# One section for the first norm and the input projection, with products behind the row conversion

## What is computed

```python
mod = jax.nn.silu(c) @ w_ada[l] + b_ada[l]
shift1, scale1, gate1, shift2, scale2, gate2 = jnp.split(mod, 6, axis=-1)
h = rms_norm(x, norm1_g[l]) * (1.0 + scale1[:, None, :]) + shift1[:, None, :]
z = h @ w_in[l]
c_q, c_kv, k_pe, dq, dk, dv = jnp.split(z, offsets, axis=-1)
```

## Time and profile before

| | us |
|---|---|
| median of 3 runs | 2666.83 (2664.89 to 2669.32) |
| the profiled execution | 2670.07 |
| its span, first to last instruction | 2668.3 |
| first matmul of the input projection | 71.6 |
| first matmul of unit 4 | 98.4 |
| end of the input projection on PE | about 276 |

### The profile page before, as it was taken

One profiled execution on the slowest core, in us unless ns is written; L12 is line 12 of the kernel. 1 busy time (PEld: TensorE's weight loads), 2 busy tenths in 40 slices (PEclk: granted clock), 3 DMA queues, 4 the chain that ended last, 5 costly groups with the idle time before them and its releaser, 6 DMA issues. The chain is left out here.

```text
span 2668.3 us, 38277 instructions
## 1 busy us (share of the span) xinstructions
PE 2487.0 (93%) x13514; PEld 1988.3 (75%) x13526; DVE 1643.6 (62%) x3033; ACT 1368.0 (51%) x2416; POOL 418.4 (16%) x530
## 2 busy tenths in 40 slices
PE   5999999999996999999994999997999899998999
PEld 4788479788765888888883778885666688886667
DVE  6663455687657999999986545420656546741761
ACT  4253244597345888888875533321666523322850
POOL 0121012320302211111112100000223200000330
PEclk7999899999997999999997999998999999999999
DMA  6642000001229999999976411033111222113211
GB/s 242 189 142 68 0 1 1 1 1 33 97 84 391 411 419 410 420 414 413 413 306 224 158 44 64 24 126 134 33 65 33 85 95 76 32 49 126 80 46 50
DMA packets 128109, 400.26 MB, mean 150 GB/s; under 512 B 12103, under 2 KB 62412, under 8 KB 115550
## 3 DMA queue, kind: packets, MB, share of 16 engines
q1 hardware_dynamic: 114522, 353.30, 35.0%
q0 software_dynamic: 12048, 42.56, 4.0%
q10 hardware_dynamic: 1396, 2.50, 0.3%
HBM read 347.93 MB, written 50.40 MB: 149 GB/s over the span
## 5 line engine op out<-in xcount | busy, mean ns | idle before, releaser
L3070 DVE CUSTOM_DVE_ANT_0 fox_l<-PS,fox_c 128x1024 f32<-128x1024 f32 (+7 forms) x128 | 92.1, 756 | 129.5 <-PE PS L3117 86.8
L3007 ACT ACTIVATE fox_l<-fox_l,stat 128x1024 f32<-128x1024 f32 (+7 forms) x128 | 98.4, 771 | 91.3 <-DVE stat L3070 90.5
L447 PE MATMUL PS<-wehg,xsTh 128*128 128x512 f32 x256 | 100.5, 392 | 3.0 <-ACT xsTh L2736 2.0
L447 PE MATMUL PS<-wehu,xsTh 128*128 128x512 f32 x256 | 103.2, 403 | 0.0
L447 PE MATMUL PS<-wqkh,uTh 128*128 128x512 f32 x256 | 103.1, 403 | 0.0
L449 PE MATMUL PS<-wqkh,uTl 128*128 128x512 f32 x256 | 100.3, 392 | 0.0
L449 PE MATMUL PS<-wehu,xsTl 128*128 128x512 f32 x256 | 100.2, 392 | 0.0
L449 PE MATMUL PS<-wehg,xsTl 128*128 128x512 f32 x256 | 100.2, 391 | 0.0
L448 PE MATMUL PS<-wqk_rest,uTh 128*128 128x512 f32 x256 | 100.0, 391 | 0.0
L449 PE MATMUL PS<-wehd,aTl 128*128 128x512 f32 x248 | 96.5, 389 | 0.0
L447 PE MATMUL PS<-wehd,aTh 128*128 128x512 f32 x248 | 96.5, 389 | 0.0
(11 more groups left out here) (610 smaller groups left out, 7499.1 us busy)
## 6 DMA issues: line engine op xcount, KB each, us to landing
we0g<-in_w_expert_gate SPq DMA_DIRECT2D x16, 2048.0 KB, 10.9
we0u<-in_w_expert_up SPq DMA_DIRECT2D x16, 2048.0 KB
we1g<-in_w_expert_gate SPq DMA_DIRECT2D x16, 2048.0 KB, 11.4
we1u<-in_w_expert_up SPq DMA_DIRECT2D x16, 2048.0 KB
we0d<-in_w_expert_down SPq DMA_DIRECT2D x16, 2048.0 KB
we1d<-in_w_expert_down SPq DMA_DIRECT2D x16, 2048.0 KB
wada_rest<-in_w_ada SPq DMA_DIRECT2D x16, 1024.0 KB, 5.7
X<-in_x SPq DMA_DIRECT2D x16, 512.0 KB, 11.6
```

Of the source, the lines that this page charges most:

```text
L447: nc.tensor.matmul(out, lh, rh, start=start, stop=False)
L3007: nc.scalar.activation(prob(p, e)[:, 0:K], prob(p, e)[:, 0:K], ACT.Exp, bias=nbm[:, u % 8:u % 8 + 1], scale=-1.0, accum_out=rsum[:, u % 16 ...
L3070: nc.vector.tensor_tensor_reduce(out=prob(p, e)[:, 0:K], in0=PS[:, 2 * e:2 * e + 2, :].rearrange("p a b -> p (a b)")[:, 0:K], in1=C[:, h % ...
```

## The change

The two sections become one (`phase_start_and_in`), so that no engine waits for the others between them, and the work in it is put in another order:

- PE no longer turns all rows ahead of the products. It turns units 0 to 3 as before (`FREE` is 4 instead of 6, in banks 4 to 7), and then runs units 0 and 1 (chunks 0 and 1 against the first half of the tokens) together, k by k: six matmuls as soon as unit k of the rows is converted, then `turn` of unit k + 4. The same for the second half. `units` lists the first four accordingly.
- ACT rounds weight chunks 0 and 1 ahead of the conversion of the rows. DVE takes their rests at the start of the conversion (first halves) and after its unit 3 (second halves).
- Loads: `X` tiles 6 and 7 go ahead of `w_ada` chunks 1 to 3, of `mats` only the identity is loaded first and the rest behind the first weight chunks, `trig` and the final gain go to SP behind later waits. `scale(2)` moves from behind chunk 3 to behind chunk 0, and the small lambda and mask operations to behind the conversion.
- Weight chunk 2 has a buffer of its own, where `X` lay, and is loaded as soon as eight units of rows are turned. Pieces 0 to 2 are loaded once all sixteen are turned. Chunks 3 and 4 are loaded after the first four units; then come pieces 3 and 4, and from chunk 5 on each chunk's load stands ahead of one or two pieces. Seven pieces instead of eight run before the rope, and `sum_after` names later units.

```diff
-            for i in range(1, NC):
-                chunk(i)
-            for t in range(6, T):
-                rows(t)
+        for t in range(6, T):
+            rows(t)
+        for i in range(1, NC):
+            chunk(i)
         load(sp, [(env.win[i], env.win_in[i], in_chunks(A)[i][0]) for i in range(2)])
+        sp.dma_start(env.mats[:, P:11 * P], A["mats"][:, P:11 * P]).then_inc(mats_in, 16)
...
-    sum_after = {2: 0, 4: 1, 6: 2, 8: 3, 12: 4, 16: 5, 20: 6, 24: 7}
+    sum_after = {5: 0, 7: 1, 9: 2, 12: 3, 15: 4, 18: 5, 21: 6, 25: 7}
...
-            for q in range(4):
-                ada(q)
-            for c in range(2, NCH):
-                sp.wait_ge(mm, 2 * (c - 1))
+        sp.wait_ge(first["turned"], KD)
+        load_in_chunk(sp, raw[2], chunks[2], second_in)
+        sp.dma_start(env.trig[:, :, :], A["trig"].rearrange("p (a s) -> p a s", a=2)).then_inc(env.trig_in, 16)
+        sp.wait_ge(first["turned"], 2 * KD)
+        for q in range(3):
+            ada(q)
+        sp.wait_ge(mm, 4)
+        for c in range(3, 5):
+            load_in_chunk(sp, raw[c], chunks[c], w_in[c % 2])
+        ada(3)
+        ada(4)
+        sp.dma_start(env.rows[:, 2, :], A["final_norm_g"].partition_broadcast(P)).then_inc(env.trig_in, 16)
+        for c in range(5, NCH):
+            sp.wait_ge(mm, 2 * (c - 1))
...
+        for n in range(2):
+            h = slice(n * HALF, (n + 1) * HALF)
+            for k in range(KD):
+                pe.wait_ge(first["split"], KD * n + k + 1)
+                for c in range(2):
+                    if n == 0 and k % 4 == 0:
+                        pe.wait_ge(w_lo01, 2 * (k // 4) + c + 1)
+                    last = split_product(nc, PS[:, 2 * n + c, :], (wh[c][:, k, :], lo_of(c)[:, k, :]),
+                                         (xh[:, k, h], xl[:, k, h]), k == 0, k == KD - 1)
+                    if k == KD - 1:
+                        last.then_inc(mm, 1)
+                if KD * n + k + first["free"] < 2 * KD:
+                    first["turn"](pe, KD * n + k + first["free"])
```

More of the change, by code:

```diff
@@ new lines, in convert_act @@
+    def convert_act(act):
+        act.wait_ge(mod_ready, 2)
+        for u in range(2 * KD):
+            if u % 2 == 0:
+                a, b = ab(u)
+                act.wait_ge(t_ready, u + 1)
+                nc.scalar.activation(part(full, u), bank(u), ACT.Identity, scale=a, bias=b).then_inc(full_act, 1)
+                act.wait_ge(full_act, u // 2 + 1)
+            else:
+                act.wait_ge(full_dve, u // 2 + 1)
+            nc.scalar.copy(part(hi, u), part(full, u)).then_inc(hi_done, 1)
@@ new lines, in on_pool, with on_act, chunk_hi @@
+    def on_pool(pool):
+        for c in range(2, NCH):
+            for part in range(2):
+                r = slice(4 * part, 4 * part + 4)
+                pool.wait_ge(w_hi, 2 * c + part + 1)
+                nc.gpsimd.tensor_tensor(lo_of(c)[:, r, :], raw[c][:, r, :], wh[c][:, r, :].bitcast(F32),
+                                        ALU.subtract).then_inc(w_lo, 1)
+    def on_act(act):
+        act.dma_start(brow[0:1, 0, :], A["b_ada"][0:1, 2 * D:3 * D]).then_inc(brow_in, 16)
+        act.dma_start(brow[0:1, 1, :], A["b_ada"][0:1, 5 * D:6 * D]).then_inc(brow_in, 16)
+        arrived = [0, 0]
+        def chunk_hi(c):
+            if c == 2:
+                act.wait_ge(second_in, 16 * len(chunks[c]))
+            else:
+                arrived[c % 2] += 16 * len(chunks[c])
+                act.wait_ge(w_in[c % 2], arrived[c % 2])
+            if c > 2:
+                act.wait_ge(mm, 2 * (c - 1))
+            for part in range(2):
+                r = slice(4 * part, 4 * part + 4)
+                nc.scalar.copy(wh[c][:, r, :], raw[c][:, r, :]).then_inc(w_hi, 1)
+        chunk_hi(0)
+        chunk_hi(1)
+        first["convert_act"](act)
+        for u, (kind, c, n) in enumerate(units):
+            act.wait_ge(mm, u + 1)
+            bank = PS[:, u % 4, :]
+            r = u - ROPE0
+            if kind == "c":
+                nc.scalar.copy(place(kind, c, n), bank).then_inc(evac, 1)
+            elif kind == "v":
+                if u < V0 + 2:
+                    act.wait_ge(rope_done, r - 1)
+                else:
+                    act.wait_ge(v_t, u - V0 - 1)
+                nc.scalar.copy(RS[:, r % 2, :], bank).then_inc(evac, 1)
+            else:
+                if r >= 2:
+                    act.wait_ge(rope_done, r - 1)
+                for b in range(4):
+                    to, frm = slice(32 * b, 32 * b + 32), slice(32 * (b ^ 1), 32 * (b ^ 1) + 32)
+                    last = nc.scalar.activation(RS[to, r % 2, :], PS[frm, u % 4, :], ACT.Copy,
+                                                scale=DQK ** -0.5 if kind == "q" else 1.0)
+                last.then_inc(evac, 1)
+            if u % 2 and u // 2 + 2 < NCH:
+                chunk_hi(u // 2 + 2)
@@ L635, in _ @@
         def _(sp):
[L636 to L660 removed]
+            first["sp"](sp)
@@ L687, in _ @@
[L687 to L710 removed]
+            first["act"](act)
@@ L712, in _ @@
+            second["act"](act)
         @block.vector
         def _(dve):
[L714 to L722 removed]
@@ L777, in _ @@
[L777 to L781 removed]
+            first["dve"](dve)
+            second["dve"](dve)
         @block.tensor
         def _(pe):
[L785 to L800 removed]
@@ L837, in _ @@
-            turn(NU - V0 - 1)
+            first["pe"](pe)
+            second["pe"](pe)
 def phase_up_projection(nc, A, env, sem):
```

653 lines of the change are left out of this document (308 added, 345 removed).

## The result

The changed kernel takes 2653.16 us (median of 5 runs, 2651.36 to 2658.52), the kernel before, timed beside it, 2666.83 (5 runs, 2663.6 to 2670.19). The ratio is 0.995, with a 95% interval of 0.9938 to 0.9961: between 10.4 and 16.5 us faster. Predicted were 2651.6 us and faster.

What follows compares the result with a forecast made beforehand. PE, nearly never idle over the span, bounds the kernel, so only its early losses can be won. Unit 4 15.7 us earlier, less a 0.5 stall, gives 15.2: 2666.83 becomes 2651.6 us, range 2646 to 2660.

Steps and rivals of the forecast that it cites:

- Loads: First stage: 1152 KB less ahead of the fourth `w_ada` chunk brings 3.05 us; conversion starts at 47.3 instead of 51.80.
- The chain to the first product: Conversion start to first product: DVE's two half rests 1.25, own unit 0.81, rest of unit 0 0.69; 2.75 us.
- Products against the conversion: First four units: PE is slower than the conversion, so it is dense from the second step on.
- The rival in which PE waits at each step: First four units bound by conversion and its round trip; unit 4 at 89.3, gain 7, 2660 us; chance 0.06.
- The transposes: First four units: twelve groups of four now stand between products on PE, 0.49 us each, 5.9 us in all.
- The lower bound of 0.35: Least price per group of transposes, counting only the group's start-to-start time; 4.2 us for twelve.
- The clock at the start: First products: 5.8 us at half clock as before, costing 2.85 us.
- The rival in which the mixed stage stays at the low clock: PE at clock 0.50 from first product to unit 4, which starts at 101.3; 2675 us; chance 0.06.
- Unit 4: Start of unit 4 on PE: 80.6 against 96.23 before, 15.7 us earlier.
- Weights of the later units: Unit 6 on PE: chunk 3, queued behind piece 2 on SP, comes late; stall of 0.5 us, between 0 and 2.
- The sum: Whole section: 15.7 us gained at unit 4 less the 0.5 stall, 15.2 us.
- The chance of 0.74: Whole kernel: probability given to the forecast, a gain of 11 to 19 us.

Runs made afterwards that it cites:

- old loads: Changed kernel with the first loads and `scale(2)` put back in their earlier order, overlap kept; 2658.22 us, ratio 0.9959.
- rests early: `chunks first` with DVE's two first half rests of weight chunks 0 and 1 moved into its wait for PE's sum; 2652.08 us, ratio 0.9938.
- turns twice: Changed kernel with each of the twelve groups of transposes between products issued twice; 2657.56 us, ratio 0.9962.
- turns first: Changed kernel without the overlap: PE turns all sixteen units and waits until all are converted before any product; 2662.37 us, ratio 0.9979.
- chunks first: Changed kernel with SP's loads of weight chunks 3 and 4 ahead of the load of piece 2; 2650.72 us, ratio 0.9937.

## Why the prediction was right, step by step

**Loads.** The forecast for the fourth chunk was 40.5, found 39.59, and the conversion started at 46.44 instead of 47.3. The gain was 5.4 us where 4.5 was booked; `old loads` gives 3.9 of it at the chunk. The term that was too small is the bytes: 1152 KB were to bring 3.05 us, and 3.9 (`old loads` against the changed kernel) to 4.0 (from the 43.58 at which I put the chunk before) came. Whether the two `X` tiles cost less than their share of the bytes or the others more is not shown. The other 1.4 us, above all `scale(2)` gone from between PE's sum and DVE's small operations, came as booked.

**The chain to the first product.** 2.75 was booked, 2.66 found (46.44 to 49.10). `rests early` shows that its parts may not be taken as if each counted alone: 1.25 us of them are worth 0.46.

**Products against the conversion.** PE is dense from the first product on, 4.00 of 4.00 us between 64 and 68. The rival in which PE waits at each step (unit 4 at 89.3) does not occur, and `turns twice` confirms that PE's own work sets the pace.

**The transposes.** 0.49 each was booked. Found: a step of 1.83 less six products, 1.36, is 0.47, 5.7 us in all instead of 5.9. Of the 0.47, 0.43 are the transposes themselves, the rest is the change between the two kinds. The lower bound of 0.35 is refuted.

**The clock at the start.** 2.85 was booked, and this was the term most off: 28.80 from the first product to unit 4, less 21.76 and 5.7, leaves 1.3. The slow pace ends within the first group of transposes: six products and that group take 3.16 us, 49.10 to 52.26, where a step at full pace takes 1.83. In the other executions of the changed kernel the same difference is 1.6 to 2.4, so it lies between a half and some four fifths of what I booked. The 5.8 us of slow pace did come in `turns first`; why it is shorter with the overlap is open. The granted clock cannot show it; it reads 1.00 from 49.10 on:

```profile
49.10:52.20 3.10, 3.10 (x9) 1.00 0.00 0
```

That is the window of PE alone, at the slow pace just named. `chunks first`, at the same slow pace (six matmuls from 50 to 52 in both), reads 0.50 from 49 to 53. The rival in which the mixed stage stays at the low clock (2675) is refuted. By the rule of the Trainium skill that I weighed ("TensorE: Matmul & The Clock Gate", Part 4), transposes do not engage the full clock. For transposes alone and with gaps, `turns first` agrees, 0.24 us each over 14 us, twice; the kernel before does not, where transposes alone reached the full pace and kept it over gaps of 0.70 us; and for groups among products it does not apply, 0.43 us for four.

**Unit 4.** 80.6 was forecast, 77.90 came: 0.95 us from the earlier first product, 1.5 from the clock, 0.2 from the transposes. So 18.3 us were gained there where 15.7 was booked.

**Weights of the later units.** The mechanism was as described: SP stood at the load of piece 2, chunk 3 was issued at 82.44 and unit 6 waited 0.77 (0.44 to 0.77 over five executions), where 0.5 was booked. The chunk's way from issue to rounding was longer than the sum had it, 6.8 us where 5.2 and up to 1.0 more were booked. `chunks first` shows the mechanism by taking the wait away. In the first profile the drop of the clock added 1.6, for which there was no term. The later pieces went as foreseen: DVE's slack shrank, and PE waited for none of them.

**The sum.** 15.2 us was forecast for the section; at its end 15.9 are found in the profiled pair and 16.8 to 18.2 in the other four executions. The medians differ by 13.7 (2666.83 to 2653.16), the ratio allows 10.4 to 16.5. So the marks give 2 to 4.5 us more than the medians. For the first pair this can be added up: its profiles lie 3.24 above and 1.80 below their medians, 5.0 together, of which 2.8 lie behind the section; the other 2.2 are in it, and 15.9 less 2.2 is 13.7. Which of the two kernels they belong to is not known with one profile of before. The forecast of 2651.6 against 2653.16 is thus partly luck: loads, clock and transposes brought 2.7 us more at unit 4 than booked, the drop and the part of the wait beyond 0.5 took 1.9 of it back in the first profile, and the medians show 1.5 us less than the forecast. The chance of 0.74 was given for a gain of 11 to 19 us, 2647.8 to 2655.8, while the range was named as 2646 to 2660; the 13.7 lie in both.

## What to carry to other kernels

When a full engine and an empty one change places in a stage, sum up the stage anew from the work of the engine that is now full, down to the small instructions that used to be hidden; here twelve groups of transposes cost 5.7 us and were the largest charge against the overlap. Then walk through every load whose consumer moves forward by as much, and read what it is queued behind in the issuing engine's list: one waiting load in front of the weights cost 0.4 to 0.8 us here, and moving it cost one line. A stall or a clock drop seen in a single profile deserves a second execution before it is explained.

## What was not expected of the hardware

- The granted clock of the record can contradict the pace. With transposes at 0.24 us each in the same 13.9 us it read 1.00 in one execution and 0.53 in another; from 50 to 52, at the start of the products, it read 1.00 in one and 0.50 in another, with six matmuls in each.
- Sixteen transposes without a gap (3.79 us) were followed by full clock, 48 of them with idle times of 0.15 to 0.7 us between groups were not, in 14 us. Once the pace had risen, groups with 0.70 us of idle time between them kept it. Why is open.
- Some 1.2 us behind an idle time of 0.77 us one execution fell to half pace, from about 93 to 96.3; after waits of 0.44 to 0.74 us in four others, and of 2.64 us in another kernel, nothing followed. Idle time alone does not decide it.
